# PEER experts of a hybrid decoder step: expert products in pairs of tokens, and one nominal time line for all five engines

## What is computed

```python
z = x @ w_in                                    # 5192 columns: conv input, q, k, v, indexer, gates
conv = silu(ln(depthwise_conv31(glu(z)))) @ w_conv_out
idx  = top_k(relu-indexer scores)               # 128 keys of 512 (prompt), 256 of 1028 (sample)
attn = softmax(q @ k[idx]) @ v[idx]
h    = ln(ALPHA * x + (sig(g_conv) * conv + sig(g_attn) * attn) @ w_out)

qh = h @ peer_w_query                           # 8 heads of 128
t1, i1 = top_k(qh1 @ keys1, 16); t2, i2 = top_k(qh2 @ keys2, 16)
ts, j = top_k(t1[:, None] + t2[None, :], 16)    # 16 experts a head, 128 a token
g = softmax(ts)
u, v = peer_u[eidx], peer_v[eidx]               # rows of 1024 numbers, from 16384 each
y = ln(ALPHA * h + sum_e g_e * gelu(h . u_e) * v_e)
```

## Time and profile before

| | |
|---|---|
| median of 3 runs | 2376.9 us (2366.78 to 2381.3) |
| the profiled execution, whole | 2361.44 us |
| its span, first to last instruction | 2359.6 us |
| TensorE matmul busy | 1725.5 us (73%) |
| VectorE busy | 1469.2 us (62%) |
| GpSimd busy (issuing fetches) | 1229.6 us (52%) |
| moved by DMA | 683.98 MB, 290 GB/s over the span |

### The profile page before, as it was taken

How to read it: one execution, slowest core, us unless ns; L and a number is a source line. 1 busy time by engine, 2 the same in 40 slices (tenths; PEclk the granted TensorE clock), 3 DMA queues, 4 the chain that set the end, 5 groups by cost and what they waited for, 6 DMA issues and landing times.

```text
span 2359.6 us, 19465 instructions
## 1 busy us (share of the span) xinstructions
PE 1725.5 (73%) x6002; PEld 643.2 (27%) x6002; DVE 1469.2 (62%) x3807; ACT 287.3 (12%) x712; POOL 1229.6 (52%) x1108
## 2 busy tenths in 40 slices
PE   7899993589814677859767887798654868599347
PEld 3454441332401122322212324122100323242011
DVE  4328957861296997668299864947699644019541
ACT  1410101121102011010101201011100112000000
POOL 1003356752315777736568874558555754336564
PEclk9999996789957898979889997898777988799778
DMA  8708899865527999859989996799987999769796
GB/s 317 308 27 306 294 390 331 305 227 199 168 81 265 331 354 378 328 189 368 364 284 316 338 356 247 271 351 351 308 267 256 336 330 338 264 232 352 280 337 252
DMA packets 215683, 683.98 MB, mean 290 GB/s; under 512 B 27637, under 2 KB 63061, under 8 KB 208979
## 3 DMA queue, kind: packets, MB, share of 16 engines
q0 software_dynamic: 157376, 581.67, 68.4%
q1 hardware_dynamic: 51195, 91.90, 11.2%
q10 hardware_dynamic: 7008, 9.17, 1.1%
HBM read 669.97 MB, written 13.10 MB: 289 GB/s over the span
## 4 chain that ended last, share of the span: by engine, by line
PE 28%; DVE 25%; issue 18%; DMA 13%; POOL 11%; SPq 3%; ACT 2%; another core or an unknown queue 0%; DVEq 0%; ACTq 0%; POOLq 0%
PE acc L1526 12%; POOL rings L779 11%; DVE rings L1879 8%; DMA rings<-peer_u,late 6%; DMA rings<-peer_v,late 4%; PE bank L1281 3%; PE wide L1220 3%; DVE small L1590 2%; PE acc L1169 2%; DVE uah L1593 2%; DVE conv_acc L1716 1%; PE wide L1526 1%; DMA w_query_s<-cache_kT 1%; PE wide L1486 1%; DVE soft_score L1593 1%
## 5 line engine op out<-in xcount | busy, mean ns | idle before, releaser
L1526 PE MATMUL acc<-rings,z_stages 128*32 128x512 f32 x2048 | 878.7, 667 | 384.4 <-DMA rings<-peer_v,late 278.6
L779 POOL DMA_INDIRECT rings<-peer_u,late x544 | 640.4, 1177 | 608.5 <-DVE late L1879 376.1
L779 POOL DMA_INDIRECT rings<-peer_v,late x544 | 580.4, 1067 | 419.3 <-PE acc L1526 267.9
L1526 PEld LDWEIGHTS acc<-rings,z_stages 128*32 128x32 f32 x2048 | 180.6, 117 | 943.9 <-issue 515.5
L1879 DVE CUSTOM_DVE_ANT_0 rings<-rings,uah 128x1024 f32<-128x1024 f32 x288 | 349.2, 1225 | 127.4 <-DMA rings<-peer_u,late 112.1
L1879 DVE CUSTOM_DVE_ANT_0 rings<-rings,late 128x1024 f32<-128x1024 f32 x256 | 310.4, 1223 | 105.8 <-DMA rings<-peer_u,late 98.8
L1202 PE MATMUL acc<-rings 128*128 128x512 f32 (+1 forms) x352 | 150.0, 577 | 0.0
L1716 DVE SCALAR_TENSOR_TENSOR conv_acc<-uah,conv_p,conv_acc 128x128 f32<-128x128 f32 x480 | 132.7, 348 | 0.0
L1650 DVE MAX8 uah<-zt 128x8 f32<-128x128 f32 (+1 forms) x80 | 22.5, 282 | 145.7 <-ACT zt L938 145.7
L1281 PE MATMUL bank<-uah,w_query_s 128*128 128x128 f32 (+1 forms) x640 | 86.5, 290 | 15.1 <-issue 15.0
L1281 PEld LDWEIGHTS bank<-uah,w_query_s 128*128 128x128 f32 x640 | 80.6, 202 | 39.0 <-issue 39.0
(11 more groups left out here) (232 smaller groups left out, 1624.3 us busy)
## 6 DMA issues: line engine op xcount, KB each, us to landing
rings<-w_in SPq DMA_DIRECT2D x36, 1024.0 KB, 6.9
rings<-peer_u,late POOLq DMA_INDIRECT x544
rings<-peer_v,late POOLq DMA_INDIRECT x544
w_query_s<-cache_kT SPq DMA_DIRECT2D x64, 128.0 KB
w_query_s<-cache_v SPq DMA_DIRECT2D x64, 128.0 KB
z_rows<-z_stages ACTq DMA_DIRECT2D x30, 256.0 KB
soft_score<-ln SPq DMA_DIRECT2D x6, 1024.0 KB
zt<-z_rows SPq DMA_DIRECT2D x2, 2596.0 KB
```

Of the source, the lines that this page charges most:

```text
L779: nc.gpsimd.indirect_dma_start(ring[:, place, :], None, table, offs).then_inc(done[place], 16)
L1526: last = nc.tensor.matmul(acc_v[QUAD * j:QUAD * (j + 1), half * BLK:(half + 1) * BLK], lone[:, quad % LONE, j, QUAD - 1 - m:2 * QUAD - 1 - m],
```

## The change

Four things.

1. **Pairs.** `expert_pair` issues two tokens together: it waits for both rows and then issues the first half of both tokens and the second half of both. The pair stands in the order where its second token stood.
2. **One time line.** Every piece on every engine has a position in nominal microseconds. `weave` and the steps are gone; `run` merges all pieces of an engine. A tile's front is laid on a table: `CLOCK_0`, `CLOCK_1`, and from tile 2 on `CLOCK_T`, begun 100 us after the step before it begins (`FRONT_LAG`); S has `CLOCK_S`. Tile 1's front begins at nominal 266 (335 before).
3. **Other fetch order.** A fetch is 1.35 nominal us. A step of tile t begins at `step_at(t)`, 345.6 us apart. It has 24 times u, v, v; then 48 times u, u, v; then the last 8 u; then the first 32 of v of tile t (64 before). Uses stand 6 us behind their fetch. Routing of a tile ends 83 us into its own step, so that its heads stand between fetches of its own u.
4. **Second pass closer.** `second_at` goes by 6.2 nominal us a half (11.6 before), `UNIT` from 11.5 to 6.1.

With it, the counters for chained VectorE instructions become one per tile, and the last layer norm (`finish`) gets a counter and a place of its own on the time line.

```diff
-    def steps():
...
-    START_T1, END_T1 = 335.0, 575.0
-    for s in range(SLOTS):
-        FETCH_AT["u", 0, s] = 168.0 + 3.0 * s if s < 34 else 270.0 + 1.3 * (s - 34)
-    for i in range(HALF):
-        FETCH_AT["v", 0, i] = 405.0 + 2.0 * i
+    MIXED_FROM, SLOT_US, LANDING = 474.0, 1.35, 6.0
+    EARLY_V, SLOW_U = P // 4, 24
+
+    def step_at(t):
+
+        return MIXED_FROM + (t - 1) * 2 * P * SLOT_US
+
+    def fetches():
+
+        for k in range(SLOTS):
+            yield 172.0 + 2.3 * min(k, 40) + 1.7 * max(k - 40, 0), ("u", 0, k)
+        for i in range(EARLY_V):
+            yield 425.0 + 1.5 * i, ("v", 0, i)
         for t in range(1, N_TILES):
...
+            order = []
+            for k in range(SLOW_U):
+                order += [("u", t, k), ("v", t - 1, EARLY_V + 2 * k), ("v", t - 1, EARLY_V + 2 * k + 1)]
+            for i in range(EARLY_V + 2 * SLOW_U, P):
+                k = SLOW_U + 2 * (i - EARLY_V - 2 * SLOW_U)
+                order += [("u", t, k), ("u", t, k + 1), ("v", t - 1, i)]
+            order += [("u", t, k) for k in range(SLOW_U + 2 * (P - EARLY_V - 2 * SLOW_U), SLOTS)]
+            order += [("v", t, i) for i in range(EARLY_V)]
+            for k, f in enumerate(order):
+                yield step_at(t) + k * SLOT_US, f
...
+    def uses():
+
+        for at, (table, tile, number) in FETCHES:
+            yield at + LANDING + (4.0 if table == "v" and number < EARLY_V else 0.0), table, tile, number
...
+    CLOCK_1 = ((0.0, 266.0), (0.05, 280.0), (0.09, 292.0), (0.2, 325.0), (0.48, 400.0), (0.497, 406.0), (0.51, 410.0),
...
+    CLOCK_T = ((0.0, 0.0), (0.05, 15.0), (0.09, 27.0), (0.2, 70.0), (0.48, 155.0), (0.497, 160.0), (0.51, 162.0),
...
+    CLOCK_S = ((0.0, 0.0), (0.04, 15.0), (0.21, 75.0), (0.48, 165.0), (0.84, 280.0), (1.18, 350.0), (1.3, 370.0))
+    FRONT_LAG, FINISH_LAG, LN2_LAG = 100.0, 305.0, 20.0
 
     def timed(pieces, t):
 
+        clock = (CLOCK_0, CLOCK_1)[t] if t < 2 else CLOCK_T if t < S_T else CLOCK_S
+        start = step_at(t - 1) + FRONT_LAG if t >= 2 else 0.0
         for x in pieces:
-            yield float(np.interp(x, *zip(*CLOCK_0))) if t == 0 else START_T1 + (END_T1 - START_T1) * x
+            yield start + float(np.interp(x, *zip(*clock)))
...
-        return 127.0 if k == 0 else 156.0 + 11.6 * (k - 1)
-
-    UNIT = 11.5
+        return 127.0 if k == 0 else 137.0 + 6.2 * (k - 1)
+
+    UNIT = 6.1
...
+    def run(*pieces):
+
+        for _ in merge(*pieces):
+            pass
...
-        weave(Strand(merge(first_pass(), second_pass(), timed(front(0), 0), timed(front(1), 1))), nothing())
-        for t in range(1, N_TILES - 1):
-            weave(Strand(front(t + 1)), nothing())
-            finish(t - 1, ln2_soft, soft[:, 0:D_MODEL])
...
+        run(first_pass(), second_pass(), *(timed(front(t), t) for t in range(N_TILES)), timed(front_sample(), S_T),
+            *(finish(t, ln2_soft, soft[:, 0:D_MODEL]) for t in range(LAST - 1)),
+            finish(LAST - 1, u_ring[:, 0:2, :], u_ring[:, 2, :]))
...
-        def expert(v, i):
-
-            place, landed, _ = v_home(v, i)
+        def expert_pair(v, i):
+
             acc_v = wide if v == S_T else acc
-            j, m = i % N_QUADS, i // N_QUADS
+            m = i // N_QUADS
             quad = sums_before(v) // N_QUADS + m
-            pe.wait_ge(v_in[place], landed)
-            if j == 0:
+            for k in (i, i + 1):
+                place, landed, _ = v_home(v, k)
+                pe.wait_ge(v_in[place], landed)
+            if i % N_QUADS == 0:
                 pe.wait_ge(diag_ready, quad + 1)
             for half in range(2):
...
+                for k in (i, i + 1):
+                    j, place = k % N_QUADS, v_home(v, k)[0]
+                    last = nc.tensor.matmul(acc_v[QUAD * j:QUAD * (j + 1), half * BLK:(half + 1) * BLK],
+                                            lone[:, quad % LONE, j, QUAD - 1 - m:2 * QUAD - 1 - m],
+                                            v_ring[:, place, half * BLK:(half + 1) * BLK], start=False,
+                                            stop=(m == tokens(v) // N_QUADS - 1), skip_group_check=True)
+                    if half:
+                        last.then_inc(summed, 1)
```

More of the change, by code:

```diff
@@ L1134, in mixer, with finishes @@
                     column(tile, number // N_QUADS)
-                if table == "v" and tile < S_T and number == P - 1:
+                if table == "v" and tile == LAST and number == P - 1:
                     finish(tile)
+        def finishes():
+            for v in range(LAST):
+                yield finish_at(v) + LN2_LAG + 2.0
+                finish(v)
         def finish(v):
@@ L1540, in mixer @@
                         weights_T(tile)
-                    expert(tile, number)
+                    if number % 2:
+                        expert_pair(tile, number - 1)
         pe.wait_ge(consts_in, 64)
         pe.wait_ge(s_zero, 5)
-        weave(Strand(merge(first_pass(), timed(front(0), 0), second_pass(), timed(front(1), 1))),
-              Strand(mixer(0)))
-        for t in range(1, N_TILES - 1):
-            weave(Strand(front(t + 1)), Strand(mixer(t)))
-        weave(Strand(front_sample()), Strand(itertools.chain(mixer(LAST), (1 + x for x in mixer(N_TILES)))))
+        run(first_pass(), second_pass(), *(timed(front(t), t) for t in range(N_TILES)), timed(front_sample(), S_T),
+            mixer())
     @block.vector
     def _(dve):
-        chain = Chain(dve, dve_chain)
+        chains = [Chain(dve, x) for x in dve_chain]
+        ln2 = Chain(dve, ln2_chain)
         V = nc.vector
@@ L1702, in taps @@
         def taps(t, lo, hi):
-            last = [0] * CC
+            chain, last = chains[t], [0] * CC
             for k in range(CONV_W):
@@ L1724, in attention @@
             n_groups, before = N_HEADS // per, att_before(t)
-            step = (hi - lo) / n_groups
+            step, chain = (hi - lo) / n_groups, chains[t]
             for g in range(n_groups):
```

162 lines of the change are left out of this document (71 added, 91 removed), and 2 rows, old and new, of the table CLOCK_0.

## The result

| | before | after |
|---|---|---|
| median | 2379.1 us (4 runs) | 2405.99 us (4 runs, 2401.64 to 2416.28) |
| ratio | 1 | 1.0129, 95% interval 1.0078 to 1.0179 |
| profiled execution, span | 2359.6 us | 2399.8 us |
| mean granted clock | 0.859 | 0.777 |

What follows compares the result with a forecast made beforehand. No engine fills the span, so it was cut into windows along the tiles' fronts. Terms 45 + 10 - 13 - 51 = -9 us put the profiled execution at 2352 and the median at 2368, range 2260 to 2440.

Steps and rivals of the forecast that it cites:

- Start and tile 1: From the start to tile 1's last head: at about 757 us, before at 712.3, so +45 us.
- Intervals: Last head of tile 1 to tile 2's, then to tile 3's: about 410 and 434 us, +10 and -13.
- price of a place: Each place where tokens break into front matmuls on TensorE: about 1.9 us saved when it disappears.
- load waits: Waits for the next z ahead of tiles 2, 3 and the sample tile: 17, 17 and about 20 us.
- Sample tile: From tile 3's last head to the sample tile's: 585 us, before 636.2, so -51 us.
- page gather and selection: In the sample tile: 102.5 + 132 us less one or two, TensorE and VectorE having the same work.
- The tail: Sample tile after its attention: 87 us less up to 25 for 13 places, taken as 16 less.
- The end: Last fetches and layer norm after the sample tile: 163.6 us, left unchanged, with the same fetches.
- Fetch pace: Faster rival, chance 0.30: fetches fill the front's gaps, both intervals run at 366 us, 2256 in all.
- Poor fill: Slower rival, chance 0.13: VectorE fills tile 1 only 0.754, +30 us, and the sample's attention gains nothing; 2414.
- sample's attention: Sample tile: 214 us less 8 (22 places for 26) to 23 (16 fetches fewer), taken as 16 less.
- Pairs save nothing: Slower rival, chance 0.12: the pair's wait for both rows eats the 1.9 us per place; 2449.

Runs made afterwards that it cites:

- e4: The kernel after with the start in the order of before (second pass, tile 1's front, first fetches); 2353.8 us, ratio to before 1.0002.
- e5: e4 with single tokens in place of pairs; 2354.1 us, ratio to before 1.0002.
- e2: The kernel after with single tokens in place of pairs, each where its own use stands on the time line; 2394.79 us, ratio to before 1.0114.
- e10: The kernel after with the second pass 19 nominal us later, nothing else; 2379.86 us, ratio to before 1.0094.
- e11: e4 once more, beside e12 on one chip; 2354.19 us, ratio to before 0.9981.
- e8: e4 with pairs for tiles 0 to 2 and single tokens for tile 3 and the sample tile; 2350.86 us, ratio to before 0.990.
- e12: e8 once more, beside e11 on one chip; 2344.2 us, ratio to before 0.9892.
- e6: The kernel after with the fronts of tiles 2 and 3 earlier on the time line; 2454.04 us, ratio to before 1.0418.
- e7: e4 with the fronts of tiles 2 and 3 earlier as in e6, and the sample tile's front earlier too; 2393.22 us, ratio to before 1.0086.
- e1: The kernel before with pairs alone, all else in the old order; 2364.71 us, ratio to before 0.9987.
- e9: e4 with one of the two matmuls of each token of tile 3 left out; 2339.69 us, ratio to before 0.9883.

## Why the prediction was wrong

The forecast was -9 us, and it came out +27 by the medians (+40 in the profiled executions), inside the range and with the sign wrong.

- **Start and tile 1, +45: right**, measured +45.2, but the closeness is luck. (Its own steps, 398 + 172 + 90 + 95, add up to 755 and +43.) z behind all weights and rotate at 396 came as forecast. The attention took 160.5 for 172, since VectorE filled 0.94 and not 0.887; the products took 99.4 for 90, the heads 101.7 for 95, and these misses cancel. The fetch ring stood still for 73 us, but at 38 fetches and behind tile 0's exponential, not at 44 behind `rotate`. e4 shows that this term decides the sign of the change: without it the ratio is 1.000.
- **Intervals, +10 and -13**, measured +11.6 and -22: near, by two errors that cancel. Products 115 and 118 came as 101.9 and 103.5, routing 96 and 97 as 108.2 and 104.2. The forecast took 6 dot products from the attention and put 19 among the heads; 15 came out of the product window, where it had no term for them. And it priced the 19 as 22 us of VectorE's work; for tile 1 it had gone by the fetches, and 71 fetches at 1.43 are 101 us. The price of a place, 1.9, was somewhat high in the products: 1.4 (e4 against e5). The load waits, taken as 17, 17 and 20, were 16.8, 24.9 and 26.1.
- **Sample tile, -51: wrong, -2.6.** This is the failed step, in three terms; without this gain tile 1's +45 is not made up. The attention, "214 less 8 (22 places for 26) to 23 (16 fetches fewer)": 215.6. The tail, "less up to 25 (13 places x 1.9) ... I take 16": 85.6 for 87. And "page gather and selection ... less one or two": 243.6 for 234.5, longer by 9. I had carried a price from product windows over to stages where an interruption less is worth almost nothing: e4 against e5 has 17 fewer in the attention for 0.9 us. In the tail, what pairs save on tokens, 6.1 us, the slower clock takes twice from the matmuls beside them. Why the gather grew is open; it isn't the pairs, since e2 with singles has 120.4 us in it (its clock is 0.79, after's 0.60).
- **The end, 0: wrong, +8.** "The same fetches; I leave it", and the pair's wait "is covered while VectorE sets the pace". In the end VectorE is busy for 53 of 172 us and does not set the pace, so the cover was gone: 170.6 to 174.7 us in four profiles with pairs on the new line (after, e4, e10, e11), 160.9, 160.9, 160.1 and 164.4 in four with singles (e2, e5, e8, e12).
- **The rivals.** Fetch pace: its intervals of 366 never came, and e6 and e7, which got 354 and 349 once, paid them back in fetches left over. Poor fill: its 2414 is the figure nearest to the measured 2406, by luck, since its main step, a fill of 0.754 at tile 1 and +30, did not happen (0.94). Its second half, nothing gained in the sample's attention, did; the clock that was to speak for it is low there, but is shown to cost time only in the tail. Pairs save nothing: right as a sum (e1 0.9987) and not in the product windows, where they do gain.

Open: why e10's attention stretched to 171 us with a DMA share of 0.78, and what besides TensorE holds the sample's attention near 246 us (243.8 to 250.5 in the profiles on the new line with full tokens, but for e7's 241.1); page loads were not varied. The clock's part is shown by matmuls of one shape at two clocks; no run sets the clock by itself.

## What to carry to other kernels

A saving on TensorE counts only in windows whose length TensorE sets. Elsewhere most of it becomes waiting (here 176 to 199 us of some 250), and a smaller part comes back as slower neighbours, so look at the busy time of the other engines and the granted clock of that window first. When work is moved along a time line, price the window that it leaves and the one that it enters, and take the fetches along with the dot products. Grouping work that waits for loads is free only while another engine sets the pace; in the last fetches, take it back to single steps (here 10 us between the medians, for one `if`). And when all later tiles hang on one chain, price a late start in full: 44 us at tile 1 were 48 at the end of the profiled executions, and the reordering downstream that was tried on that start (e6) recovered none of them.

## What was not expected of the hardware

- The mean granted clock of the whole kernel follows the way tokens are issued and hardly anything else: 0.757 to 0.8 in the ten profiles with pairs (e8's, e12's and e9's among them), 0.856 to 0.868 in the four with singles or padding, also between kernels of the same time (e4 and e5: 2353.8 and 2354.1 us).
- Between those two, 204 us less TensorE work (1542.2 and 1745.9 busy) changed the time by nothing, and the matmuls that are the same in both took 892 us for 847.
- In one stage of one kernel the granted clock was 0.70 in one profile and 0.85 in another, and the stage took 59.6 and 50.0 us (e8 and e12).
